# One recurrent head norm taken with tokens on partitions and spread over the features by TensorE, one step later

## What is computed

```
q, key, log_f, v = chunks(q, K), chunks(key, K), chunks(log_f, K), chunks(v, V)
b = jnp.cumsum(log_f, axis=3)
q_dec = q * jnp.exp(b)
k_dec = key * jnp.exp(-b)
a = jnp.where(causal, jnp.einsum('bhcid,bhcjd->bhcij', q_dec, k_dec), 0.0)
o_intra = jnp.einsum('bhcij,bhcje->bhcie', a, v)
...
o_inter = jnp.einsum('bhcid,cbhde->bhcie', q_dec, states)
o = (o_intra + o_inter).transpose(0, 2, 3, 1, 4).reshape(B, S, H, V)
o = o * lax.rsqrt(jnp.mean(o * o, axis=-1, keepdims=True) + RMS_EPS) * norm_g.astype(F32).reshape(H, V)
```

## Time and profile before

| | us |
|---|---|
| median of 3 runs | 2394.69 |
| lowest and highest run | 2393.44, 2396.1 |
| profiled execution, span of its trace | 2404.0 |
| TensorE busy in it | 2185.2 (91%) |
| VectorE busy in it | 1310.8 (55%) |
| ScalarE busy in it | 911.0 (38%) |

### The profile page before, as it was taken

One profiled execution on the slowest core, in us unless ns is written; L12 is line 12 of the kernel. 1 busy time (PEld: TensorE's weight loads), 2 busy tenths in 40 slices (PEclk: granted clock), 3 DMA queues, 4 the chain that ended last, 5 costly groups with the idle time before them and its releaser, 6 DMA issues.

```text
span 2404.0 us, 29078 instructions
## 1 busy us (share of the span) xinstructions
PE 2185.2 (91%) x10758; PEld 1755.2 (73%) x10758; DVE 1310.8 (55%) x1983; ACT 911.0 (38%) x1307; POOL 91.7 (4%) x99
## 2 busy tenths in 40 slices
PE   5758879999997999999996899999899977999996
PEld 3645567888885788888885678888678765888885
DVE  6675556443445556566655743244467867433444
ACT  4203324222224655655562442142254534322422
POOL 1000030000030000000001000000000000000000
PEclk9877899999999999999997899999989989999998
DMA  3100122223222222222211132222111211322221
GB/s 140 45 1 27 42 98 70 100 80 117 81 94 79 88 76 84 76 83 69 78 64 41 69 105 89 103 88 99 68 53 61 70 55 68 105 88 93 99 88 52
DMA packets 32090, 185.50 MB, mean 77 GB/s; under 512 B 4737, under 2 KB 5121, under 8 KB 13313
## 3 DMA queue, kind: packets, MB, share of 16 engines
q1 hardware_dynamic: 27216, 176.17, 21.3%
q10 hardware_dynamic: 2736, 6.00, 0.7%
q0 software_dynamic: 2048, 2.17, 0.4%
HBM read 180.06 MB, written 2.10 MB: 76 GB/s over the span
## 4 chain that ended last, share of the span: by engine, by line
PE 79%; DVE 11%; DVEq 4%; ACT 3%; issue 2%; ACTq 0%; DMA 0%; POOL 0%; POOLq 0%
PE ps L504 12%; PE ps L506 12%; PE ps L505 12%; PE ps L849 5%; PE ps L851 5%; PE ps L850 5%; PE ps L891 3%; PE ps L893 3%; PE ps L892 3%; PE ps L527 1%; PE ps L529 1%; PE ps L528 1%; DVE f_run L2174 1%; PE ps L668 1%; PE ps L787 1%
## 5 line engine op out<-in xcount | busy, mean ns | idle before, releaser
L504 PE MATMUL ps<-x_hi,w_lo 128*128 128x512 f32 x928 | 365.0, 393 | 20.2 <-DVE u L1656 13.8
L505 PE MATMUL ps<-x_lo,w_hi 128*128 128x512 f32 x928 | 363.2, 391 | 0.0
L506 PE MATMUL ps<-x_hi,w_hi 128*128 128x512 f32 x928 | 363.1, 391 | 0.0
L1024 ACT ACTIVATE w_hi<-raw 128x2048 fp32r<-128x2048 f32 x122 | 232.8, 1908 | 284.4 <-PE ps L506 223.6
L1427 DVE TENSOR_TENSOR w_lo<-raw,w_hi 128x2048 fp32r<-128x2048 f32 x122 | 280.0, 2295 | 99.0 <-ACT w_hi L1024 98.5
L849 PE MATMUL ps<-x_hi,w_lo 128*128 128x512 f32 x560 | 225.1, 402 | 6.4 <-DVE w_lo L1997 6.4
L504 PEld LDWEIGHTS ps<-x_hi,w_lo 128*128 128x128 f32 x928 | 175.6, 189 | 60.5 <-issue 15.1
L851 PE MATMUL ps<-x_hi,w_hi 128*128 128x512 f32 x560 | 219.5, 392 | 0.0
L850 PE MATMUL ps<-x_lo,w_hi 128*128 128x512 f32 x560 | 218.6, 390 | 0.0
L505 PEld LDWEIGHTS ps<-x_lo,w_hi 128*128 128x128 f32 x928 | 175.7, 189 | 36.7 <-issue 0.2
L506 PEld LDWEIGHTS ps<-x_hi,w_hi 128*128 128x128 f32 x928 | 175.5, 189 | 36.9
(11 more groups left out here) (403 smaller groups left out, 3869.5 us busy)
## 6 DMA issues: line engine op xcount, KB each, us to landing
raw<-w_attn_in SPq DMA_DIRECT2D x32, 1024.0 KB, 4.9
raw<-w_gate_up SPq DMA_DIRECT2D x22, 1024.0 KB, 4.9
raw<-w_up_a SPq DMA_DIRECT2D x16, 1024.0 KB, 4.9
raw<-w_down_a SPq DMA_DIRECT2D x16, 1024.0 KB, 4.9
raw<-w_up_h SPq DMA_DIRECT2D x16, 1024.0 KB, 4.8
raw<-w_down_h SPq DMA_DIRECT2D x16, 1024.0 KB, 4.9
raw<-w_hgrn_in SPq DMA_DIRECT2D x8, 1024.0 KB, 5.0
raw<-w_down SPq DMA_DIRECT2D x8, 768.0 KB, 4.2
```

The lines of the kernel that those rows point to most:

```text
L504: pe.matmul(o, w_lo[:, slot, a:a + P], hi[:, k, :], start=k == 0, stop=False)
L505: pe.matmul(o, w_hi[:, slot, a:a + P], lo[:, k, :], start=False, stop=False)
L506: last = pe.matmul(o, w_hi[:, slot, a:a + P], hi[:, k, :], start=False, stop=k == st.kc - 1)
L1024: act.activation(w_hi[:, slot, :], raw[:, slot, :], ACT.Copy).then_inc(whi_ready, 1)
```

## The change

The sum of squares is now taken with the squares as the stationary operand and a column of ones moving: four matmuls with one column each, one for each block of 128 tokens (`TB` is 4). Bank 5 then holds 128 by 4 numbers, tokens on partitions. ScalarE's root and VectorE's reciprocal are of 128 by 4 elements (`root4`, `rstd4`). A new function `spread_head` turns the reciprocal back: four matmuls of 128 columns with a column of `rstd4`, repeated 128 times, as stationary operand and the identity moving. VectorE copies the 128 by 512 result out of PSUM and multiplies as before. `spread_head` of head `a - 1` stands in step `hd` behind the first two chunks of tile 0 (in steps 2 to 7), at the start of step 8 for head 6, and at the end of step 8 for head 7. The wait of TensorE for `oh_ready` moves ahead of the key-value products.

```diff
+            def spread_head(a):
+                pe.wait_ge(rstd_ready, SK_ROOT["head0"] + a + 1)
+                for b in range(TB):
+                    last = pe.matmul(ps[:, 5, b * P:(b + 1) * P], rstd4[:, b:b + 1].to_broadcast([P, P]), ident,
+                                     start=True, stop=True)
+                last.then_inc(head_spread, 1)
...
                 if project:
-                    hgrn_tile(hd, par, 0, range(DC))
+                    if attend and not (isinstance(a, int) and a == 0):
+                        hgrn_tile(hd, par, 0, range(2))
+                        spread_head(a - 1)
+                        hgrn_tile(hd, par, 0, range(2, DC))
+                    else:
+                        hgrn_tile(hd, par, 0, range(DC))
+                else:
+                    spread_head(a - 1)
                 if attend:
                     pe.wait_ge(dec_ready, a + 1)
...
                     pe.wait_ge(ht_ready, a + 1)
-                    pe.wait_ge(root_ready, SK["head0"] + a)
+                    if not (isinstance(a, int) and a == 0):
+                        pe.wait_ge(oh_ready, a)
...
                     pe.wait_ge(a_ready, a + 1)
-                    if not (isinstance(a, int) and a == 0):
-                        pe.wait_ge(oh_ready, a)
...
                     pe.wait_ge(sq_ready, SB["head0"] + a + 1)
-                    pe.matmul(ps[:, 5, :], ones, sq[:, 0, :], start=True, stop=True).then_inc(sq_used, 1)
+                    for b in range(TB):
+                        last = pe.matmul(ps[:, 5, b:b + 1], sq[:, 0, b * P:(b + 1) * P], one, start=True, stop=True)
+                    last.then_inc(sq_used, 1)
                     if not project:
                         out_slab(range(5, DC - 1))
+                        spread_head(a)
...
-                    act.activation(root[:, :], ps[:, 5, :], ACT.Sqrt, bias=eps[:, 0:1], scale=1.0 / P) \
+                    act.activation(root4, ps[:, 5, 0:TB], ACT.Sqrt, bias=eps[:, 0:1], scale=1.0 / P) \
...
                     dve.wait_ge(root_ready, SK["head0"] + a + 1)
-                    dve.reciprocal(rstd[:, :], root[:, :]).then_inc(rstd_ready, 1)
+                    dve.reciprocal(rstd4, root4).then_inc(rstd_ready, 1)
+                    dve.wait_ge(head_spread, a + 1)
+                    dve.tensor_copy(rstd[:, :], ps[:, 5, :])
```

More of the change, by code:

```diff
@@ L193, in build @@
     ident, swap1, ones = (consts[:, n, :] for n in range(3))
+    one = consts[:, 2, 0:1]
     ident_b = extra("ident_b", [P], bf16)
@@ L209, in build @@
     rstd = extra("rstd", [T])
+    by_token = extra("by_token", [2, TB])
     tmp = extra("tmp", [4, T])
@@ L255, in build @@
     SUM, MEAN = 7, 6
+    root4, rstd4 = (by_token[:, n, :] for n in range(2))
     def counts(rows):
@@ L320, in build @@
     rstd_ready = sem("rstd_ready")
+    head_spread = sem("head_spread")
     x_ready = [sem("x_ready0"), sem("x_ready1")]
```

## The result

The changed kernel takes 2436.51 us (median of 4 runs, 2435.14 to 2437.78) against 2395.39 us before (4 runs, 2393.44 to 2403.28). The ratio is 1.0166, with a 95% interval of 1.0147 to 1.0185: 1.7% slower, 41.1 us by the medians. The forecast was 2441.3 us, with a range of 2426 to 2455.

What follows compares the result with a forecast made beforehand. A cycle of waits between TensorE, nearly the bound, and VectorE was taken to bound the kernel. The terms 32.4 + 13.2 + 0.5 + 0.5 = 46.6 us on 2394.7 gave 2441.3 us, range 2426 to 2455.

Steps and rivals of the forecast that it cites:

- The cycle and the stall: Tile 0, steps 2 to 7: TensorE stands still some 4.6 us for the small reciprocal behind `k_dec`, six chunks queued.
- The price without the clock: Steps 2 to 7: signal and reciprocal, spread and six chunks uncovered, 5.4 us a step, 32.4 us in all.
- The 1.00 us: Spread's four matmuls in tile 0: 1.00 us, read from the start of L945 to that of L951.
- The 0.85 us: Spread in tile 0: eight weight loads at 107 ns each, an estimate from the skill page, against the row's 1.00.
- The clock: Behind each of six stalls the granted clock falls for 4.5 us, half lost: 2.2 us a step, 13.2 in all.
- The 1.6 us read from step 1: Price of the slow stretch behind step 1's 2.20 us idle time; by it the clock term is 9.6 us.
- Work in the shadow: Loop: smaller root and reciprocal, new sum of squares and VectorE's wait for the spread are each worth 0.
- Step 8 and the end: Head 6's spread ahead of L945 costs 0.5 us; head 7's, queued behind the output chunks, 0.5 us.
- The one without a fall of the clock: Rival for the loop: same stall, no loss of clock, 33.4 us, 2428 us; chance 0.12.
- Slow stretches of 9 us: Rival for the loop: same stall, slow stretches of 9 us or more each, 60.4 us, 2455 us; chance 0.10.
- The case of nothing: Rival for tile 0: loads and chunks slip ahead of the wait and fill the stall, 2395 to 2401 us; chance 0.04.
- The faster one: Rival: the spread waits for nothing, reciprocals in steps 7 to 8 and the end shrink, 2389.7 us; chance 0.03.

Runs made afterwards that it cites:

- the first two experiments: Changed kernel, spread behind all eight chunks of tile 0: 2402.92 us; changed kernel, small reciprocal ahead of the large reciprocal of the decays: 2399.22 us.
- the filled stall: Changed kernel plus 18 unneeded matmuls of 512 columns ahead of the spread's wait in steps 2 to 7; 2426.81 us, ratio 1.0140.
- the first experiment: Changed kernel with the spread behind all eight chunks of tile 0 instead of two, in steps 2 to 7; 2402.92 us, ratio 1.0034.
- the third's: Kernel before plus four float32 matmuls with a repeated column of ones behind two chunks of tile 0, without any wait; 2399.20 us, ratio 1.0013.

## Why the prediction was right

The sum was 32.4 us without the clock, 13.2 for the clock and 1.0 for step 8 and the end. The traces show 30.6, 11.0 and -0.2, 41.4 in all. Each term was too high, so none made up for another.

*The cycle and the stall.* Right, shown by the first two experiments: TensorE waits in tile 0 for a reciprocal that stands behind `k_dec`, with six chunks queued behind the wait. It waited 4.4 us; 4.6 was forecast.

*The price without the clock.* 5.4 us a step forecast; the filled stall shows 5.1 (30.6 for six against 32.4). The rows of that run give the parts: the spread 0.92 us to the next chunk instead of 1.00, the six chunks 4.17 us, and no 0.08 us for the change to the products (L966 there), which start 0.22 us behind their forerunner. The 1.00 us was the distance from L945 to the transposes; it depends on what follows. Behind a like wait the spread took 0.99 us to the products of `k_dec` in the first experiment and 0.92 to a chunk here. The 0.85 us, an estimate worked out from the Trainium skill, page "TensorE: Matmul & The Clock Gate", section LDWEIGHTS, was no further off than the 1.00: the runs show 0.90 to 0.92. The small reciprocal is 0.17 us and moves the start by 0.09 us, measured from the start of `k_dec` (1881.53 to 1882.42, before 1869.57 to 1870.37).

*The clock.* The mechanism was right: behind each of the six stalls the granted clock fell. The size was off. I took 2.2 us a step, it was 1.4 to 2.1, 11.0 us in all instead of 13.2. The 1.6 us read from step 1 was the nearer value. Its slow stretch was as good a model as any, and I went above it for a stall twice as long, without a row for that. PEclk was 0.89 to 0.94 where about 0.85 was forecast. In the step of the rows above the slow stretch is as long as I took it, 4.5 us: TensorE ran at half rate from 1882.42 to about 1886.9. That step lost 2.1 us (30.77 against 28.63 with the filled stall). The Trainium skill, page "TensorE: Matmul & The Clock Gate", Part 1, puts the loss at half of such a stretch, an estimate of 2.2 us here, and the trace agrees.

*Work in the shadow.* The root, the sum of squares and VectorE's wait for the spread cost nothing, as forecast. The sum of squares is 1.23 us from its start to the second matmul behind it (1.20 before). VectorE's 2.4 us less of work a step is worth nothing in the loop: its idle time grew. One sign came out otherwise: VectorE waits 6.7 us a step for the key-value products, not 8 to 10, and the rest of its idle time stands elsewhere, 2.9 to 3.5 us ahead of the mask and 1.6 to 2.2 ahead of the copy.

*Step 8 and the end.* This step of the sum failed, in a small way. I had 1.0 us of loss, and it was 0.2 us of gain. The way to step 8 grew by 1.8 us (25.43 against 23.63), but what follows shrank by 2.0 (24.60 against 26.62). I had compared the key-value products with the mask and kept the mask at its old time. The mask stands behind the product of head 6 and seven splits, and all of them came 2.2 us earlier after the products of `k_dec`, since the large reciprocal was gone ahead of them. The second half, the last head's spread queued behind the output chunks, was as forecast, but at half the size: 5.48 us from the sum of squares to the product, 5.23 before. The 2.0 us is one pair of traces in a stretch that varies by 1 us; the sign is borne out by the other pair, 48.9 us for the first experiment's end against 49.3 for the third's.

*The rivals.* The one without a fall of the clock is what the filled stall measured, 2426.81 us where 2428 stood. Slow stretches of 9 us didn't come; the one above was 4.5. The case of nothing fell with the idle time: no chunk slipped ahead of the wait. The faster one was right about its mechanism and wrong about its condition. Where the spread waits for nothing, the ends of the layer gain and the loop pays 0.4 us a step; only the kernel that uses it for the last two heads alone is clearly below before.

## What to carry to other kernels

A wait is as dear as what is queued behind it on the waiting engine: find the instruction that it waits for, see what stands ahead of that on its own engine, and count the matmuls between the wait and the next thing that another engine needs. A smaller instruction saves nothing while it keeps its place in a queue behind a long one. And a cheaper form of a step may pay only where the step is on the path: the one kernel here that is faster than before uses it for the last two of eight heads, together with two changes of order.

## What was not expected of the hardware

Doing useless work in an idle time made the kernel 9.7 us faster, since the granted clock then stayed at 1.00. The clock fell behind idle times of 2.4 to 2.6 us in four steps of six and behind 4.4 to 4.6 us in six of six. The loss was 1.4 to 2.6 us behind the shorter ones and 1.4 to 2.1 behind the longer, so the same stall has not one price, and a longer one wasn't dearer. Four float32 matmuls of one moving column (eight instructions) take as long as one of 512 columns (two instructions): 1.23 and 1.20 us to the second matmul behind. So a float32 matmul shows as two instructions at one column too, not only at 128 and more; the weights and activations of the tiles, split into high and low parts, show as one.
